# Making a block's weight low half before, and not after, the fetched row on VectorE

## The chip, the cores and the metric

One core of one Trainium2 chip runs the whole program. The metric is device time in microseconds (us) for one execution. TensorE is called PE in the profile, VectorE DVE, ScalarE ACT, GpSimd POOL and SyncE SP.

## What is computed

The program is two transformer blocks on 512 tokens of width 1024. The change lies in the last layer of the second one, a product-key mixture of 16384 experts (`peer`):

```
expert, gate: per token, 8 heads x 16 best of N_EXPERTS = 128 * 128
ub = u_tab[expert]; vb = v_tab[expert]          # rows of 1024
a  = gelu(einsum('td,ted->te', x, ub))          # 128 numbers per token
y  = einsum('te,ted->td', gate * a, vb)
```

The result is added to the residual stream.

## The kernel before

**Two ways to do the experts.** For tokens 0 to 383 the kernel multiplies the tokens with all 16384 rows of `peer_u`, in 128 blocks x of 128 experts each, and weighs the result with a gate matrix that is zero where a token did not choose an expert; a later stage multiplies the weighed result with `peer_v`. The last 128 tokens (one per partition) take the literal way: POOL fetches, for each of the 128 choices, the row of `peer_u` that each token chose (one indirect DMA into a ring `gathered` of NGATHER = 4 buffers), and DVE forms the dot product (`use_row`, L2308). Rows 128 to 255 are the rows of `peer_v`, which DVE adds up (L2316).

**Split weights.** Every block of weights arrives by SP's DMA in `wraw` (3 buffers), ACT makes its high half `WH` (L1191), and another engine its low half `WL = wraw - WH`. PE needs both and does three matmuls for each product (L469, L472, L473), 24 for one `u` block. From block FIRST_GATE_UP = 33 on, DVE makes the low halves (`low`, L2297); it must find the cast done (semaphore `w_hi`) and PE begun with the block two ahead of it in order (`w_begun`). PE waits for `WL` in `unit_views`; SP waits for the low half of unit u-3 before it reloads that `wraw` buffer.

**The gate stage** has blocks x = 33 to 127. In 64 of the first 86 of them PE also makes the gate matrices for four tokens (`gm`, L951) from one-hot matrices that DVE builds in two instructions (`hots_of`, L2329 and L2333). DVE's program is one loop over x, in a fixed order: one-hots for block x+1, one row, low half of block x+2. Two rows (EARLY = 2) are used ahead of the loop, so that 97 rows are used in this stage. Behind the loop `weigh(0)`, `weigh(1)` and `low_weighed(0)` prepare the first operands of the next stage, `down`.

**POOL's queue** is in one order too: a fetch of a row (L1160), then 0, 1 or 2 scatters of gate values to the gate matrices in DRAM (L1151; 128 in all, 16 over 11 rows), then the next fetch. Fetch r waits until row r-4 is used (`rows_used`). After the last scatter POOL loads four gate matrices, which `weigh` needs.

Of the kernel before, what the change touches and what calls it, by code (L numbers as in the profile page):

```python
# [68 lines left out]
FIRST_GATE_UP = 2 * PH * UP_BY_PART + UP_BEFORE_SEL + UP_AFTER_SEL  # L69
LAST_GATE_UP = FIRST_GATE_UP + GATE_UPS  # L70
NGATHER = 4
EARLY = 2
# [15 lines left out]
def fours_of(x):  # L88

    b = x - FIRST_GATE_UP  # L90
    if not 0 <= b < GATE_UPS:
        return range(0)
    fours = NFOUR - FIRST_FOUR
    return range(FIRST_FOUR + b * fours // GATE_UPS, FIRST_FOUR + (b + 1) * fours // GATE_UPS)


def rows_until(slot):

    ups = NEXP - FIRST_GATE_UP
    after = min(slot, GATE_UPS) + max(min(slot, ups) - GATE_UPS, 0)   # L100
    rest = 2 * HS - EARLY - ups
    return EARLY + after + min(max(slot - ups, 0) * rest // (NEXP - 4), rest)
# [34 lines left out]
def block_pair_kernel(nc, A, onehot_rows, inv_freq, out):  # L137

    ctx = ExitStack()
    with ctx:  # L140
# [5 lines left out]
        def s(name):  # L146
            if name not in sems:
                sems[name] = ctx.enter_context(nc.semaphore(name))
            return sems[name]
# [8 lines left out]
        def wait_full(eng, key):  # L158
            n = number[key]
            eng.wait_ge(s(f"full{n % 8}"), n // 8 + 1)  # L160
            return banks[n % 8]

        def wait_read(eng, key):

            n = number[key]
            eng.wait_ge(s(f"free{n % 8}"), n // 8 + 1)
# [6 lines left out]
        unit_at = {}  # L173
# [1489 lines left out]
        def _(dve):  # L1663
            links = [0]

            def link(ins):

                links[0] += 1
                ins.then_inc(s("dve_link"), 1)
                dve.wait_ge(s("dve_link"), links[0])  # L1670
# [619 lines left out]
            def low(u, made=s("w_low")):  # L2290
                if u >= len(units):
                    return
                k, n, _ = units[u]
                dve.wait_ge(s("w_hi"), u + 1)
                if u >= NW:
                    dve.wait_ge(s("w_begun"), u - NW + 2)
                dve.tensor_tensor(WL[:, u % NW, 0:k * n], wraw[:, u % NR, 0:k * n],  # L2297
                                  WH[:, u % NW, 0:k * n].bitcast(F32), ALU.subtract).then_inc(made, 1)

            def use_row(row):  # L2300
                dve.wait_ge(s(f"row_landed{row % NGATHER}"), 16 * (row // NGATHER + 1))
                at = gathered[:, row % NGATHER, :]
                if row == 0:
                    dve.wait_ge(s("x_nat_made"), 1)
                if row == HS:
                    dve.wait_ge(s("gates_copied"), 1)
                if row < HS:
                    dve.tensor_tensor_reduce(out=at, in0=at, in1=x_nat[:, :], scale=1.0, scalar=0.0, op0=ALU.mult, op1=ALU.add,  # L2308
                                             accum_out=gdot[:, row:row + 1]).then_inc(s("rows_used"), 1)
                    return  # L2310
                for n, (first, end) in enumerate(((0, UP_ROWS_1), (UP_ROWS_1, UP_ROWS_2))):
                    if row - HS == first:
                        dve.wait_ge(s("rows_active"), n + 1)
                        link(dve.tensor_tensor(gdot[:, first:end], gdot[:, first:end], ggate[:, first:end], ALU.mult))
                dve.wait_ge(s("rows_used"), row)
                dve.scalar_tensor_tensor(out=hN[:, NTD, :], in0=at, scalar=gdot[:, row - HS:row - HS + 1],  # L2316
                                         in1=hN[:, NTD, :], op0=ALU.mult, op1=ALU.add).then_inc(s("rows_used"), 1)

            def use_rows(slot):
                for row in range(rows_until(slot), rows_until(slot + 1)):  # L2320
                    use_row(row)

            def gate_matrices():
                def hots_of(x):
                    for four in fours_of(x):
                        if four >= FIRST_FOUR + NQ:
                            wait_full(dve, ("gm", four - NQ))
                        q, tok = four % NQ, slice(four * TOK4, (four + 1) * TOK4)
                        link(dve.tensor_tensor(hots[:, q, :, :, :],  # L2329
                                               iota128[:, :].unsqueeze(1).unsqueeze(1).to_broadcast([P, 2, TOK4, P]),  # L2330
                                               ijcol[:, :, tok].unsqueeze(3).to_broadcast([P, 2, TOK4, P]),
                                               ALU.is_equal))
                        dve.tensor_tensor(hots[:, q, 0, :, :], hots[:, q, 0, :, :],  # L2333
                                          gcol[:, tok].unsqueeze(2).to_broadcast([P, TOK4, P]), ALU.mult).then_inc(
                                              s("hots_made"), 1)

                low(LOW_BY_DVE)
                for t in range(TSCAT // P, NTD):
                    wait_read(dve, ("sel", t))
                hots_of(FIRST_GATE_UP)  # L2340
                low(LOW_BY_DVE + 1)
                for row in range(EARLY):
                    use_row(row)
                for x in range(FIRST_GATE_UP, NEXP):
                    hots_of(x + 1)
                    use_rows(x - FIRST_GATE_UP)
                    low(unit_at[("u", x)] + 2)
                for x in range(2):
                    weigh(x)
                low_weighed(0)  # L2350

            def weigh(x):
                dve.wait_ge(s(f"ag_landed{x % NAG}"), sum(32 if NAG <= n < SENT else 16 for n in range(x % NAG, x + 1, NAG)))
                if x < NAG:
                    dve.wait_ge(s("first_gates_landed"), 16 * NAG)
                if x >= 2:
                    dve.wait_ge(s("ga_lo"), x - 1)
                if x >= SENT:
                    wait_read(dve, ("a", x))
                if x == 0:  # L2360
                    for four in range(TSTAY // TOK4, NFOUR):
                        wait_read(dve, ("gm", four))
                a = ar[:, x % NAG, :] if x < SENT else kept[:, x - SENT, :]
                dve.tensor_tensor(ga[:, x % 2, 0:TSTAY], a[:, 0:TSTAY], gr[:, x % NAG, :], ALU.mult)
                dve.tensor_tensor(ga[:, x % 2, TSTAY:TD].rearrange("p (a t) -> p a t", a=NGSTAY),
                                  a[:, TSTAY:TD].rearrange("p (a t) -> p a t", a=NGSTAY), Gs[:, :, x, :],
                                  ALU.mult).then_inc(s("ga"), 1)

            def low_weighed(x):
                dve.wait_ge(s("ga_hi"), x + 1)  # L2370
                dve.tensor_tensor(GL[:, x % NGA, :], ga[:, x % 2, :], GH[:, x % NGA, :].bitcast(F32),
                                  ALU.subtract).then_inc(s("ga_lo"), 1)
# [24 lines left out]
            rows_and_norm(2, "norm2")  # L2397
            choose_experts()
            gate_matrices()
            down()  # L2400

# [56 lines left out]
```

## Time and profile before

| what | value |
|---|---|
| median of 3 runs | 2169.43 us |
| lowest, highest | 2164.5, 2172.26 us |
| span of the profiled execution | 2161.6 us |
| outside the span, to the median | 7.8 us |
| PE busy | 2121.7 us (98%) |
| DVE busy | 1442.4 us (67%) |
| POOL busy | 1038.6 us (48%) |
| gate stage in the profile | about 1166 to 1635.58 us |

The profiled execution has no time of its own in the results; its span covers the first to the last instruction, and the median stands 7.8 us above it. In a timeline row, the start and the duration of an instruction are followed by its engine, line, operation and tiles; in brackets stand the engine's idle time before it and what ended it.

### The profile page before, as it was taken

Reading aid. Unit: us, or ns where it says so; the run is one execution under the profiler, and the core shown is the slowest. Engines: PE = TensorE matmul, PEld = TensorE weight load, DVE = VectorE, ACT = ScalarE, POOL = GpSimd, SP = SyncE. Lnnn points to the kernel's source line nnn. Section 1 sums busy time; section 2 is a strip of 40 time slices with the busy share of each in tenths; the row PEclk is TensorE's granted clock in tenths of the full one; section 3 lists DMA queues with packets and bytes.
Section 4 is the critical chain, followed back from the end, with each engine's and each line's share of the span. In section 5 each row is a group of like instructions: output and inputs, shape, how many; then the busy total and the mean of one; then the engine's idle time right before and its main releaser. Section 6 shows DMA issues by size and latency. Waiting matters only on the chain.

```text
span 2161.6 us, 29125 instructions
## 1 busy us (share of the span) xinstructions
PE 2121.7 (98%) x10648; PEld 1837.8 (85%) x10648; DVE 1442.4 (67%) x2713; ACT 858.3 (40%) x1306; POOL 1038.6 (48%) x573
## 2 busy tenths in 40 slices
PE   8989999999999999999999999999999999999999
PEld 7857888888877877899999999999998888888887
DVE  5973411110054995369998777787867999999987
ACT  4354522232264454253334444444433333333332
POOL 1203244443423333435566888888863444444342
PEclk9999999999999999999999999999999999999999
DMA  4202344444442222334347899998899999999996
GB/s 177 82 27 62 104 117 127 117 119 115 117 118 74 86 71 77 117 106 121 112 147 207 242 267 321 284 315 249 261 309 318 388 388 371 373 375 377 369 359 251
DMA packets 240489, 444.14 MB, mean 205 GB/s; under 512 B 102459, under 2 KB 152028, under 8 KB 240220
## 3 DMA queue, kind: packets, MB, share of 16 engines
q1 hardware_dynamic: 152060, 299.07, 41.8%
q0 software_dynamic: 55488, 134.83, 19.3%
q10 hardware_dynamic: 32800, 8.39, 1.8%
q8 instruction: 85, 1.39, 0.3%
q14 instruction: 56, 0.46, 0.1%
HBM read 397.71 MB, written 44.50 MB: 205 GB/s over the span
## 4 chain that ended last, share of the span: by engine, by line
PE 69%; POOL 13%; DVE 8%; issue 4%; DMA 3%; ACT 2%; SPq 0%; DVEq 0%; ACTq 0%; POOLq 0%
PE bank L469 22%; PE bank L473 22%; PE bank L472 22%; POOL gate_matrices L1151 9%; POOL y L1160 4%; DMA y<-in_peer_u_rows,gidx 3%; DVE m L1979 1%; PE bank L923 1%; DVE xn L1980 1%; DVE WL L2297 1%; PE bank L645 1%; DMA wraw<-in_peer_u 1%; ACT sc L1302 1%; DVE y L2308 0%; DVE hots L2329 0%
## 5 line engine op out<-in xcount | busy, mean ns | idle before, releaser
L1140 POOL TENSOR_TENSOR WL<-wraw,WH 128x1024 fp32r<-128x1024 f32 x171 | 435.9, 2552 | 723.5 <-ACT WH L1191 723.5
L1191 ACT ACTIVATE WH<-wraw 128x1024 fp32r<-128x1024 f32 x411 | 435.0, 1060 | 627.4 <-PE bank L469 393.6
L469 PE MATMUL bank<-XH,WH 128*128 128x384 f32 (+2 forms) x1864 | 668.8, 359 | 12.6 <-DVE WL L2297 7.8
L473 PE MATMUL bank<-XH,WL 128*128 128x384 f32 (+2 forms) x1864 | 657.8, 353 | 0.0
L472 PE MATMUL bank<-XL,WH 128*128 128x384 f32 (+2 forms) x1864 | 657.6, 353 | 0.0
L469 PEld LDWEIGHTS bank<-XH,WH 128*128 128x128 f32 x1864 | 351.4, 189 | 46.3 <-issue 12.9
L472 PEld LDWEIGHTS bank<-XL,WH 128*128 128x128 f32 x1864 | 351.6, 189 | 29.0 <-issue 0.7
L473 PEld LDWEIGHTS bank<-XH,WL 128*128 128x128 f32 x1864 | 351.1, 188 | 28.7
L2297 DVE TENSOR_TENSOR WL<-wraw,WH 128x1024 fp32r<-128x1024 f32 x240 | 293.0, 1222 | 57.6 <-ACT WH L1191 51.8
L469 PE MATMUL bank<-WH,GH 128*128 128x512 f32 x768 | 298.9, 389 | 1.6 <-issue 1.6
L473 PE MATMUL bank<-WH,GL 128*128 128x512 f32 x768 | 298.8, 389 | 0.0
L472 PE MATMUL bank<-WL,GH 128*128 128x512 f32 x768 | 298.8, 389 | 0.0
L1160 POOL DMA_INDIRECT y<-in_peer_v,gidx x128 | 185.2, 1447 | 220.7 <-DVE hN L2316 203.0
L1151 POOL DMA_INDIRECT gate_matrices<-scat_gate,scat_at x128 | 243.7, 1904 | 40.9 <-issue 38.4
L2308 DVE CUSTOM_DVE_ANT_0 y<-y,x_nat 128x1024 f32<-128x1024 f32 x128 | 156.0, 1223 | 108.6 <-DMA y<-in_peer_u_rows,gidx 103.4
L1160 POOL DMA_INDIRECT y<-in_peer_u_rows,gidx x128 | 169.3, 1323 | 106.1 <-DVE gdot L2308 77.0
L469 PEld LDWEIGHTS bank<-WH,GH 128*128 128x128 f32 x768 | 144.1, 188 | 32.3 <-issue 2.3
L473 PEld LDWEIGHTS bank<-WH,GL 128*128 128x128 f32 x768 | 144.1, 188 | 29.9
L472 PEld LDWEIGHTS bank<-WL,GH 128*128 128x128 f32 x768 | 144.2, 188 | 29.8
L2316 DVE SCALAR_TENSOR_TENSOR hN<-y,gdot,hN 128x1024 f32<-128x1024 f32 x128 | 163.9, 1280 | 3.6 <-DMA y<-in_peer_v,gidx 0.6
L1589 ACT ACTIVATE ac<-bank 128x384 f32<-128x384 f32 x122 | 59.8, 490 | 239.0 <-PE bank L473 223.6
L1904 DVE TENSOR_TENSOR y<-bank,y 128x512 f32<-128x512 f32 x22 | 15.2, 692 | 208.2 <-PE bank L473 208.2
(313 smaller groups left out, 2561.8 us busy)
## 6 DMA issues: line engine op xcount, KB each, us to landing
wraw<-in_peer_u SPq DMA_DIRECT2D x128, 512.0 KB
wraw<-in_peer_v SPq DMA_DIRECT2D x128, 512.0 KB
activations<-ac SPq DMA_DIRECT2D x122, 192.0 KB
ar<-activations SPq DMA_DIRECT2D x122, 192.0 KB
gr<-gate_matrices SPq DMA_DIRECT2D x124, 128.0 KB
wraw<-in_w_gate SPq DMA_DIRECT2D x22, 512.0 KB
wraw<-in_w_up SPq DMA_DIRECT2D x22, 512.0 KB
wraw<-in_w_down SPq DMA_DIRECT2D x22, 512.0 KB
```

Of the source, the lines that this page charges most:

```text
L469: mm = pe.matmul(out, wh, xh, start=first, stop=False)
L472: pe.matmul(out, wh, xl, start=False, stop=False)
L473: return pe.matmul(out, wl, xh, start=False, stop=last)
L645: mm = pe.matmul(out[half, (h % 4) * P:(h % 4 + 1) * P], v1[:, b - 1 + kt, half], pT1[:, h, kt, :], start=kt == kts[0], stop=kt == 1)
L1140: pool.tensor_tensor(WL[:, u % NW, 0:m], wraw[:, u % NR, 0:m], WH[:, u % NW, 0:m].bitcast(F32), ALU.subtract).then_inc(s("w_lo"), 1)
L1151: pool.indirect_dma_start(out=gate_cells[:, :], out_offset=bass.IndirectOffsetOnAxis(ap=scat_at[:, k:k + 1], axis=0), in_=scat_gate[:, k:k ...
L1160: pool.indirect_dma_start(out=gathered[:, row % NGATHER, :], out_offset=None, in_=(u_rows if row < HS else v_rows)[:, :], in_offset=bass.I ...
L1191: act.activation(WH[:, u % NW, 0:k * n], wraw[:, u % NR, 0:k * n], ACT.Copy).then_inc(s("w_hi"), 1)
L1589: act.activation(ac[:, x % NAC, :] if x < SENT else kept[:, x - SENT, :], src[:, 0:TD], ACT.Gelu_apprx_tanh).then_inc(frees(("a", x)), 1)
L2297: dve.tensor_tensor(WL[:, u % NW, 0:k * n], wraw[:, u % NR, 0:k * n], WH[:, u % NW, 0:k * n].bitcast(F32), ALU.subtract).then_inc(made, 1)
L2308: dve.tensor_tensor_reduce(out=at, in0=at, in1=x_nat[:, :], scale=1.0, scalar=0.0, op0=ALU.mult, op1=ALU.add, accum_out=gdot[:, row:row + ...
L2316: dve.scalar_tensor_tensor(out=hN[:, NTD, :], in0=at, scalar=gdot[:, row - HS:row - HS + 1], in1=hN[:, NTD, :], op0=ALU.mult, op1=ALU.add) ...
```

## The change

In each pass of the loop the low half of block x+2 is made before the row and no longer after it. The two early rows, ahead of the loop before, are now used in the first pass, behind its low half. No instruction is added or removed, and the other engines' programs are the same.

```diff
                 hots_of(FIRST_GATE_UP)
                 low(LOW_BY_DVE + 1)
-                for row in range(EARLY):
-                    use_row(row)
                 for x in range(FIRST_GATE_UP, NEXP):
                     hots_of(x + 1)
+                    low(unit_at[("u", x)] + 2)
+                    if x == FIRST_GATE_UP:
+                        for row in range(EARLY):
+                            use_row(row)
                     use_rows(x - FIRST_GATE_UP)
-                    low(unit_at[("u", x)] + 2)
                 for x in range(2):
                     weigh(x)
                 low_weighed(0)
```

## Rows read from the trace of the kernel before

**Rows 1.** The page's chain that ended last, by engine.

```profile
PE 69%; POOL 13%; DVE 8%; issue 4%; DMA 3%; ACT 2%; SPq 0%; DVEq 0%; ACTq 0%; POOLq 0%
```

**Rows 2.** Busy time by stretch: stretch, us, engines busy (instructions), PEclk, DMA share, GB/s.

```profile
1166.00:1595.00 429.00, 423.78 (x2612) 422.85 (x2610) 324.51 (x395) 198.37 (x244) 361.11 (x217) 1.00 0.94 273
...
1640.00:2161.00 521.00, 518.35 (x2286) 428.60 (x2284) 470.58 (x698) 186.00 (x254) 221.89 (x154) 1.00 0.97 361
```

**Rows 3.** Waits from 1166 to 1595 us: total us, times, longest us.

```profile
DVE y L2308 <- DMA y<-in_peer_u_rows,gidx: 96.3, 56, 5.6
...
PE bank L469 <- DVE WL L2297: 5.2, 4, 2.4
...
POOL y L1160 <- DVE gdot L2308: 4.0, 13, 0.3
...
DVE WL L2297 <- ACT WH L1191: 0.7, 1, 0.7
```

**Rows 4.** Timeline of DVE, one pass of the loop.

```profile
1315.12 1.23 DVE L2308 CUSTOM_DVE_ANT_0 y<-y,x_nat 128x1024 f32<-128x1024 f32 x1 [1.72 <-DMA y<-in_peer_u_rows,gidx]
...
1316.27 1.22 DVE L2297 TENSOR_TENSOR WL<-wraw,WH 128x1024 fp32r<-128x1024 f32 x1
1317.41 1.22 DVE L2329 TENSOR_TENSOR hots<-iota,sq 128x1024 f32<-128x1024 f32 x1
...
1319.32 1.21 DVE L2308 CUSTOM_DVE_ANT_0 y<-y,x_nat 128x1024 f32<-128x1024 f32 x1
```

**Rows 5.** Timeline of PE, starts of blocks and of the next stage.

```profile
1209.43 0.49 PE L469 MATMUL bank<-XH,WH 128*128 128x384 f32 x1 [2.38 <-DVE WL L2297]
...
1317.64 0.41 PE L469 MATMUL bank<-XH,WH 128*128 128x384 f32 x1 [0.49 <-DVE WL L2297]
...
1322.70 0.42 PE L469 MATMUL bank<-XH,WH 128*128 128x384 f32 x1
...
1603.08 0.41 PE L469 MATMUL bank<-XH,WH 128*128 128x384 f32 x1 [0.73 <-DVE WL L2297]
...
1635.58 0.47 PE L469 MATMUL bank<-WH,GH 128*128 128x512 f32 x1 [1.63 <-issue]
```

**Rows 6.** Instruction groups from 1166 to 1595 us, POOL's two.

```profile
L1151 POOL DMA_INDIRECT gate_matrices<-scat_gate,scat_at x128 | 243.7, 1904 | 40.9 <-issue 38.4 <-DMA gate_matrices<-scat_gate,scat_at 2.5
...
L1160 POOL DMA_INDIRECT y<-in_peer_u_rows,gidx x89 | 117.6, 1321 | 30.3 <-issue 22.9 <-DVE gdot L2308 4.0 <-DVE gidx L2277 3.5
```

**Rows 7.** Timeline of DVE at the stage's end.

```profile
1600.56 1.22 DVE L2308 CUSTOM_DVE_ANT_0 y<-y,x_nat 128x1024 f32<-128x1024 f32 x1 [5.14 <-DMA y<-in_peer_u_rows,gidx]
...
1601.71 1.22 DVE L2297 TENSOR_TENSOR WL<-wraw,WH 128x1024 fp32r<-128x1024 f32 x1
...
1628.28 1.22 DVE L2308 CUSTOM_DVE_ANT_0 y<-y,x_nat 128x1024 f32<-128x1024 f32 x1
...
1631.29 1.23 DVE L2297 TENSOR_TENSOR WL<-wraw,WH 128x1024 fp32r<-128x1024 f32 x1 [1.79 <-ACT WH L1191]
1633.28 0.42 DVE L2364 TENSOR_TENSOR ga<-ar,gr 128x256 f32<-128x256 f32 x1 [0.76 <-issue]
...
1634.92 0.56 DVE L2371 TENSOR_TENSOR GL<-ga,GH 128x384 fp32r<-128x384 f32 x1 [0.48 <-ACT GH L1637]
```

**Rows 8.** Timeline of ACT: the cast that the low half at 1601.71 needs.

```profile
1600.24 1.06 ACT L1191 ACTIVATE WH<-wraw 128x1024 fp32r<-128x1024 f32 x1 [5.05 <-DMA wraw<-in_peer_u]
```

**Rows 9.** Busy time by stretch, columns as in Rows 2: the block after the longest stall.

```profile
1209.00:1213.00 4.00, 3.57 (x12) 3.60 (x13) 3.97 (x6) 1.06 (x1) 3.39 (x3) 0.58 0.79 151
```

**Rows 10.** Timeline of POOL: a scatter beside a low half, scatter and fetch beside idle DVE.

```profile
1239.43 2.54 POOL L1151 DMA_INDIRECT gate_matrices<-scat_gate,scat_at  x1 [0.31 <-issue]
...
1245.79 1.55 POOL L1151 DMA_INDIRECT gate_matrices<-scat_gate,scat_at  x1 [0.30 <-issue]
1247.64 1.00 POOL L1160 DMA_INDIRECT y<-in_peer_u_rows,gidx  x1 [0.30 <-issue]
```

**Rows 11.** Timeline of DVE at the first of these scatters.

```profile
1239.32 1.21 DVE L2297 TENSOR_TENSOR WL<-wraw,WH 128x1024 fp32r<-128x1024 f32 x1
```

## The prediction

> **What bounds the kernel now.** I read first the busy time by stretch. PE is busy for 423.78 of 429 us while the gate stage's scatters run, and for 518.35 of 521 us in the last stage [rows 2]. So PE sets the end, the last stage follows PE's own pace, and an edit in the gate stage is worth what it takes from PE's gaps there, plus what it does to the moment at which the last stage starts.
>
> Then the waits of that stretch. PE waited 4 times for a low half, 5.2 us in all, while DVE waited 96.3 us for fetched rows [rows 3]. The low half stands behind the row on DVE, so a late row makes a late low half. The timeline shows one such case: the row is there at 1315.12, its low half starts at 1316.27, and PE starts the block at 1317.64 after 0.49 us idle [rows 4, 5]. From row to low half it is 1.15 us, from the start of the low half to PE 1.37 us, and 2.52 us in all.
>
> Last, who sets the pace of the rows. The chain of waits gives POOL 13% of the span [rows 1], although it is busy for half of it. In the 429 us POOL's two kinds of instruction are busy for 243.7 + 117.6 us, and nearly all of the 71.2 us before them is a fixed issue gap: its waits for a used row are 4.0 us in 13 pieces of 0.3 us, which is that same gap [rows 3, 6]. So POOL's queue is full from 1166 to 1595 us, the rows come at its pace, and PE, a little faster, is dragged by it whenever a row is late. This is why the four stalls cannot simply be added up as a gain.
>
> **The change part by part.** *Low half ahead of the row, in the steady loop.* The same instructions run. A low half now waits for the row of the pass before, and one-hots stand between them. After the row at 1315.12 would come its 1.15 us, then the one-hots, 1.91 us (1317.41 to 1319.32), then the low half of the block that PE starts at 1322.70 [rows 4, 5]. That block could begin at 1315.12 + 1.15 + 1.91 + 1.37 = 1319.55, so it has 3.15 us to spare, where its forerunner had none. The general form: one block period with gates, 5.06 us (1317.64 to 1322.70), less 1.91 us. A block without gates has no one-hots, and the room is larger. With the rows coming when they did, PE can therefore run 3.15 us earlier and no more before it waits for the rows again. I take 3.15 us as the gain at 1595 us. Its ends: nothing, if some other input of PE has no room; and all that the stalls cost there, 5.2 us plus the slow block after the longest of them. That block shows a granted clock of 0.58 over 4 us, so mostly the lower level of 1.2 GHz, after PE had been idle for 2.38 us [rows 5, 9]; (1 - 0.58) x 4 = 1.7 us. The upper end is 6.9 us.
>
> *The rows themselves* move back by one low half, up to 1.15 us. In this stretch that costs nothing: POOL asks for row r-4 before it fetches row r, and does not wait for it beyond its issue gap [rows 3]. That cover is gone only after 1595 us, where no scatter is left and POOL has time to spare. *SP's reload* of a `wraw` buffer waits for a low half, which comes no later, so the streams are not delayed. *What a low half newly queues:* the row, and with it POOL's ring, now stand behind its wait for the cast. Over the 429 us that wait was met once, for 0.7 us [rows 3]. *The two early rows* go behind the low half of block 35 and the first stall goes with them; it is one of the four and is already in the sum.
>
> *The end of the scatters.* A row arrives at 1600.56, its low half starts at 1601.71 and PE is stalled until 1603.08 [rows 5, 7]. The cast was started at 1600.24 and takes 1.06 us [rows 8]; a low half behind the cast alone could start at 1601.33. It gains 0.4 us.
>
> *The last pass.* Here the change costs. Before: row at 1628.28, the low half waits for its cast until 1631.29, then `weigh(0)` after 0.76 us in which DVE only issues waits, and PE starts the last stage at 1635.58 after a stall of 1.63 us, right behind the low weighed half at 1634.92 [rows 5, 7]. Afterwards the last row, which had lain in DVE's idle time ahead of that cast, stands between the low half and `weigh(0)`. Nothing hides it, because PE is already waiting for this chain: +1.15 us, and the stall becomes 2.8 us. The SP loads behind `weigh(0)` and the next stage's start all move with it, so it is counted once.
>
> Sum: -3.15 - 0.4 + 1.15 = -2.4 us. Against the profiled span: 2161.6 - 2.4 = 2159.2; with the 7.8 us that the median stands above the span, 2167.0 us.
>
> **The rivals.**
>
> *The clock falls before the last stage.* The stall of 2.8 us is longer than the one of 2.38 us after which the clock was at 1.2 GHz; the one of 1.63 us was followed by matmuls at full pace. If it falls for as long, it costs 1.7 us again [rows 5, 9]: 2168.7 us. The Trainium skill ("TensorE: Matmul & The Clock Gate", Part 1) has the clock gate slow PE when it has been idle, and the case at 1209.43 agrees. By that rule the last stage would start slow and the time would be this rival's; since only one stall here shows it, and others of 1.63 us do not, I give it less than even.
>
> *POOL's pace changes, against us.* A scatter that starts 0.1 us into a low half takes 2.54 us, one beside an idle DVE 1.55 us [rows 10, 11]. The means are 1.904 us for 128 scatters and 1.321 us for 89 fetches, against 1.55 and 1.00 us for the undisturbed: 128 x 0.35 + 89 x 0.32 = 45 + 28 = 73 us of POOL's queue is stretch that depends on how its instructions fall on DVE's [rows 6, 10]. Now the order on DVE is one-hots, low half, row. If a POOL instruction leaves the one-hots and meets the low half more often, the rows slow down and PE, which has only the room worked out above, slows with them one for one. The low half adds as much blocking as before, which speaks against it; the fact that the two blockers lay back to back, and now lie 0.7 us apart (1.91 less the 1.22 us of the first one-hot instruction) [rows 4], speaks for it. One more stretch of 1 us at every eighth of the 88 rows is 11 us: -2.4 + 11 = +8.6, 2178 us. It turns a gain to a loss from 2.4 us on, and beyond 0.3% from 8.9 us on, an eighth of the stretch there is.
>
> The Trainium skill speaks on this ("SBUF — State Buffer", the sections on ports): a DVE instruction with two SBUF inputs holds off a GpSimd one that reads SBUF, whichever comes second. By that rule the row instruction would hold POOL off as well, DVE's order would hardly matter, and this rival's extra would be nothing; the trace agrees for the low half.
>
> *POOL's pace changes, for us.* The same in the other direction. With 3.8 us or more taken from the queue the stalls all go and PE gains the whole 6.9 us: -6.9 - 0.4 + 1.15 = -6.1, 2163.3 us. It can't go much further, since nothing else of PE's time is touched.
>
> *The moved low half brings nothing.* PE's stalls could fall back on another input (the cast, a late stream), and only the cost at the end stays: +1.15, 2170.6 us. Against it: DVE waited for a cast once in this stretch, and the rows explain each stall.
>
> **How the numbers follow.** The forecast, 2167.0 us, has 42%; the clock 20% (2168.7); POOL's pace shorter 14% (2163.3); no gain 10% (2170.6); POOL's pace longer 14% (from 2170 to 2178). The least and greatest of the likely cases are 2163.3 and about 2172; the three runs shown differ by 7.8 us, so I add about 2 us on either side: 2161.5 to 2174.0. It leaves out the upper part of the slow rival and a little below. A measurement can tell some 0.3%, 6.5 us, from no change. Faster by more needs nearly the whole 6.1 us and luck in the medians: 11%. Slower by more is the upper part of POOL's longer pace: 13%. Within: 76%.
>
> **What would show it right or wrong.** PE's waits for the low half between 1166 and 1595 us should vanish for block 35 and sum up to some 2 to 4 us less with the slow block gone; PE's last stage should start 2 to 3 us earlier, near 1633 us, behind a stall of 2.8 us and not 1.63 us, with the row right in front of `weigh(0)`. The last scatter should stand within a few us of where it stood; if it moved by more, POOL's pace decides the result. The scatter and fetch means should stay near 1.90 and 1.32 us. I am wrong if POOL's waits for used rows appear before 1595 us, if the low halves wait for casts there, or if the last stage no longer keeps PE's own pace.

## The result, and the profile after

The changed kernel takes 2156.55 us (median of 14 runs, 2153.34 to 2160.82), the kernel before 2164.71 us on the same chip (14 runs, 2161.49 to 2177.38). The ratio is 0.9948, 95% interval 0.9935 to 0.9961: 0.5% faster. The forecast was 2167.0 us with a range of 2161.5 to 2174.0, and faster had a chance of 0.11. The prediction was wrong.

In the runs here the time is 1.7 to 2.2 us above the span, in most of them 1.9 to 2.1; the profiled run of the changed kernel took 2159.24 us with a span of 2157.3. The "7.8 us that the median stands above the span" was therefore about 2 us outside the span and nearly 6 us of difference between runs: three runs had given a median of 2169.43, fourteen give 2164.71.

The chain of waits has lost its POOL part, 13% before [rows 1]:

```profile
PE 89%; DVE 7%; ACT 2%; DMA 1%; issue 1%; SPq 0%; DVEq 0%; ACTq 0%
```

Busy time by stretch, columns as in [rows 2]. The scatters now end at 1589 us, and PE is busy for the whole of 424.00 us while they run; the last stage is as it was:

```profile
1166.00:1590.00 424.00, 424.00 (x2630) 423.96 (x2629) 326.51 (x398) 199.01 (x246) 355.83 (x218) 1.00 0.95 278
...
1635.00:2156.00 521.00, 518.52 (x2287) 428.85 (x2285) 469.94 (x698) 186.42 (x254) 227.65 (x154) 1.00 0.97 361
```

The waits up to 1590 us. PE's line of [rows 3], 5.2 us for low halves, has no successor. DVE waits less for rows (81.0 us, 96.3 before), and the low halves wait for casts 9 times where they did once, since DVE now gets ahead:

```profile
DVE y L2308 <- DMA y<-in_peer_u_rows,gidx: 81.0, 48, 4.4
...
DVE WL L2297 <- ACT WH L1191: 13.6, 9, 4.6
...
POOL y L1160 <- DVE gdot L2308: 1.2, 4, 0.3
```

POOL's two groups from 1166 to 1595 us. Scatters last as long as before (1904 ns), fetches 74 ns less than 1321 [rows 6]:

```profile
L1151 POOL DMA_INDIRECT gate_matrices<-scat_gate,scat_at x128 | 243.9, 1906 | 40.7 <-issue 38.1 <-DMA gate_matrices<-scat_gate,scat_at 2.6
...
L1160 POOL DMA_INDIRECT y<-in_peer_u_rows,gidx x90 | 112.2, 1247 | 27.8 <-issue 25.6 <-DVE gdot L2308 1.2 <-DVE gidx L2277 0.7
```

The first fetch and the last scatter of POOL's list, in the timeline of the kernel before and then of the changed one. From the start of the one to the end of the other it is 1593.46 - 1166.13 = 427.3 us before and 1589.04 - 1168.01 = 421.0 us after:

```profile
1166.13 1.16 POOL L1160 DMA_INDIRECT y<-in_peer_u_rows,gidx  x1 [3.49 <-DVE gidx L2277]
...
1591.38 2.08 POOL L1151 DMA_INDIRECT gate_matrices<-scat_gate,scat_at  x1 [0.30 <-issue]
```

```profile
1168.01 1.16 POOL L1160 DMA_INDIRECT y<-in_peer_u_rows,gidx  x1 [0.67 <-DVE gidx L2277]
...
1586.70 2.34 POOL L1151 DMA_INDIRECT gate_matrices<-scat_gate,scat_at  x1 [0.30 <-issue]
```

The end of the stage: PE's first matmul of the last stage, then DVE, then ACT, of the changed kernel:

```profile
1630.74 0.47 PE L469 MATMUL bank<-WH,GH 128*128 128x512 f32 x1 [1.63 <-issue]
...
1626.46 1.23 DVE L2297 TENSOR_TENSOR WL<-wraw,WH 128x1024 fp32r<-128x1024 f32 x1 [1.79 <-ACT WH L1191]
1627.60 1.22 DVE L2308 CUSTOM_DVE_ANT_0 y<-y,x_nat 128x1024 f32<-128x1024 f32 x1
...
1628.74 0.42 DVE L2365 TENSOR_TENSOR ga<-ar,gr 128x256 f32<-128x256 f32 x1
...
1630.08 0.56 DVE L2372 TENSOR_TENSOR GL<-ga,GH 128x384 fp32r<-128x384 f32 x1
...
1629.15 0.49 ACT L1589 ACTIVATE kept<-bank 128x384 f32<-128x384 f32 x1 [2.72 <-PE bank L473]
1629.53 0.98 ACT L1637 ACTIVATE GH<-ga 128x384 fp32r<-128x384 f32 x2
```

I measure the whole stage from DVE's `gidx` instruction (L2277), which starts the fetches, to this matmul: 470.0 us before (1165.55 to 1635.58), 463.3 us after (1167.43 to 1630.74), 6.7 us less. The profiled run of the changed kernel reached the stage 1.9 us later than that of before.

PE's busy time in these two stretches, before and then after (columns as in [rows 2]), parts the 6.7 us: 5.2 us less idle (470.03 - 461.32 = 8.7 us before, 463.31 - 459.80 = 3.5 us after) and 1.5 us less work, which fits the one spell at the lower clock that the kernel before had here:

```profile
1165.55:1635.58 470.03, 461.32 (x2823) 459.37 (x2823) 348.25 (x429) 212.56 (x264) 377.58 (x233) 1.00 0.93 279
```

```profile
1167.43:1630.74 463.31, 459.80 (x2832) 458.89 (x2831) 348.11 (x429) 212.59 (x265) 371.26 (x233) 1.00 0.94 282
```

### The profile page after: what moved, and what is told of

Same layout as the page of the kernel before. It is cut to its first block, busy times and chain, and to the rows that moved or that the text cites. A ratio compares the mean times of both kernels' runs of the same rounds, so it can differ in the third digit from the quotient of the medians.

```text
span 2157.3 us, 29125 instructions
## 1 busy us (share of the span) xinstructions
PE 2123.1 (98%) x10648; PEld 1840.5 (85%) x10648; DVE 1439.8 (67%) x2713; ACT 858.0 (40%) x1306; POOL 1039.3 (48%) x573
## 4 chain that ended last, share of the span: by engine, by line
PE 89%; DVE 7%; ACT 2%; DMA 1%; issue 1%; SPq 0%; DVEq 0%; ACTq 0%
PE bank L469 27%; PE bank L473 27%; PE bank L472 27%; PE bank L951 3%; DVE m L1979 1%; DMA wraw<-in_peer_u 1%; PE bank L645 1%; PE bank L923 1%; DVE xn L1980 1%; ACT sc L1302 1%; PE bank L860 0%; DMA wraw<-in_w_in 0%; DVE sc L1838 0%; DVE isc L1980 0%; PE bank L592 0%
## 5 line engine op out<-in xcount | busy, mean ns | idle before, releaser
L1160 POOL DMA_INDIRECT y<-in_peer_v,gidx x128 | 189.7, 1482 | 212.7 <-DVE hN L2316 196.5
L1160 POOL DMA_INDIRECT y<-in_peer_u_rows,gidx x128 | 163.9, 1281 | 104.2 <-DVE gdot L2308 75.5
```

Of the source, the lines that this page charges most:

```text
L1160: pool.indirect_dma_start(out=gathered[:, row % NGATHER, :], out_offset=None, in_=(u_rows if row < HS else v_rows)[:, :], in_offset=bass.I ...
```

## The experiments

Two theories stood against each other at first. By A, my prediction's own, the low half had no room behind its row, and room is what the new order gives. By B, the order of the blocking instructions on DVE sets POOL's pace. Later ones sharpen B to C, given below.

**Where in the order the gain lies.** The first runs part the change in two and move the low half further.

The loop's new order, with the early rows left ahead of the loop:

```diff
+                for row in range(EARLY):
+                    use_row(row)
                 for x in range(FIRST_GATE_UP, NEXP):
                     hots_of(x + 1)
                     low(unit_at[("u", x)] + 2)
-                    if x == FIRST_GATE_UP:
-                        for row in range(EARLY):
-                            use_row(row)
                     use_rows(x - FIRST_GATE_UP)
```

> The loop's new order, with the two early rows left ahead of the loop as before. Theory A (the low half no longer waits for the row of its own pass, so PE's stalls behind late rows go): nearly the whole gain, 6 to 8 us below the kernel before; the first stall (1.70 us at block 35) shrinks too, because the low half of block 35 no longer waits for row 2. Theory B (the gain comes from the first pass, where the early rows stood in front of everything): at most 2 us.

Only the first pass changed, the other passes as before:

```diff
-                    low(unit_at[("u", x)] + 2)
                     if x == FIRST_GATE_UP:
+                        low(unit_at[("u", x)] + 2)
...
                     use_rows(x - FIRST_GATE_UP)
+                    if x > FIRST_GATE_UP:
+                        low(unit_at[("u", x)] + 2)
```

> Only the first pass is changed (low half of block 35, then rows 0, 1 and 2); every later pass keeps the row in front of the low half. Theory A: the first stall of 1.70 us goes, but the rows still come at POOL's pace and PE meets them at the next block, so 0 to 2 us are gained and waits of 3 to 5 us for the low half remain. Theory B: 6 to 8 us gained.

The low half first of all, ahead of the one-hots (the order is low half, one-hots, row):

```diff
-                    hots_of(x + 1)
                     low(unit_at[("u", x)] + 2)
+                    hots_of(x + 1)
```

> Order low half, one-hots, row: the low half has 1.9 us more room than in the changed kernel, but low half and one-hots lie back to back on DVE again, as before the change. Theory A1 (room alone): as fast as the changed kernel or up to 1 us faster, no waits of PE for a low half before 1595 us. Theory A2 (part of the gain is POOL's shorter queue, since the two operations that hold POOL off no longer lie back to back): POOL needs 427 us from its first fetch to its last scatter as before, instead of 421 us; PE still has room (3.15 + 1.9 us), so that only 1 to 2 us of the gain are lost.

The changed kernel once more:

> The changed kernel once more, for a second profile beside the others on one chip. Both theories: 7 to 11 us below the kernel before. If POOL's shorter queue (421 us) is an effect of the order it is there again, within 2 us; if it was chance, it lies anywhere between 420 and 430 us. PE's stall before the last stage is 1.63 us again, because ACT's cast for that stage stands behind the eviction of block 127.

| run | median (range), us | ratio, 95% interval | POOL's list, us | stage, us |
|---|---|---|---|---|
| e1, loop only | 2157.72 (2154.12 to 2161.19) | 0.9957 (0.9942 to 0.9972) | 421.2 | 464.3 |
| e2, first pass only | 2166.74 (2160.1 to 2176.37) | 0.9998 (0.9979 to 1.0017) | 427.0 | 472.5 |
| e3, low half first | 2170.25 (2161.44 to 2173.4) | 1.001 (0.9991 to 1.0029) | 432.0 | 477.0 |
| e4, changed kernel | 2158.07 (2153.63 to 2162.79) | 0.9962 (0.995 to 0.9975) | 420.9 | 463.9 |

"POOL's list" is the stretch from the first fetch to the end of the last scatter. The whole gain is the loop's order; the early rows bring nothing that the runs can tell (e1 against e4). And e3 speaks against A: the low half is earliest there and PE never waits for it up to 1595 us, yet nothing is gained. By itself it doesn't settle A, for its waits up to 1595 us show that the stall went to another input, the one-hots, which are now last before the row; e6 below does:

```profile
PE bank L951 <- DVE hots L2333: 8.3, 7, 2.2
```

**The row first.** The next runs repeat the kernel before, turn the loop to row, one-hots, low half, and take POOL out of the way by leaving out every second scatter.

The kernel before once more, one run:

> The kernel before, profiled again. It tells which stalls are of the kernel and which of one execution. Theory A: 4 to 7 us of waits of PE for low halves before 1595 us, most of it in the first ten blocks, and at least one spell of halved clock behind one of over 2 us. POOL from its first fetch to its last scatter: 425 to 430 us if the order sets it.

The row ahead of the one-hots:

```diff
+                for row in range(EARLY):
+                    use_row(row)
                 for x in range(FIRST_GATE_UP, NEXP):
+                    use_rows(x - FIRST_GATE_UP)
                     hots_of(x + 1)
                     low(unit_at[("u", x)] + 2)
-                    if x == FIRST_GATE_UP:
-                        for row in range(EARLY):
-                            use_row(row)
-                    use_rows(x - FIRST_GATE_UP)
```

> Order row, one-hots, low half: the low half waits for the row of its own pass and for the one-hots, 1.9 us later than in the kernel before. Theory A: the dragging by the rows grows by what was 3.15 us of room in the changed kernel, turned round: 2 to 4 us slower than the kernel before, PE waits for low halves of 6 to 10 us. Theory B (room plays no part, the order only changes how POOL falls on DVE): within 1 us of the kernel before.

Half of the scatters left out, in the kernel before and in the changed one:

```diff
+                if k % 2:
+                    return
...
-                    pool.wait_ge(s("scattered"), 16 * k)
+                    pool.wait_ge(s("scattered"), 8 * k)
...
-                    pool.wait_ge(s("scattered"), 16 * HS)
+                    pool.wait_ge(s("scattered"), 8 * HS)
```

> The kernel before with every second scatter left out (64 of 128), so that POOL has some 140 us to spare in the stage; the gate matrices of the first 128 tokens lack half their entries. Theory A: the rows are never late, PE waits for no low half, and the time falls by 6 to 8 us, to that of the changed kernel. Rival (rows are late because of the DMA engines' load, not POOL's queue): waits for low halves of 3 us or more remain.

> The changed kernel with every second scatter left out in the same way. Theory A: with POOL out of the way the order is worth nothing: within 1 us of the kernel before with half its scatters. If the new order has a price of its own at the end of the stage (the prediction's 1.15 us), it shows here alone, as 1 us slower than that one.

| run | median (range), us | ratio, 95% interval | POOL's list, us | stage, us |
|---|---|---|---|---|
| e5, kernel before | 2175.19, one run | | 436.6 | 484.6 |
| e6, row first | 2158.76 (2154.76 to 2166.4) | 0.9958 (0.9939 to 0.9977) | 421.2 | 466.4 |
| e7, before, half scatters | 2155.7 (2153.48 to 2161.09) | 0.9937 (0.9914 to 0.9961) | 402.0 | 467.5 |
| e8, changed, half scatters | 2156.14 (2153.51 to 2161.14) | 0.9946 (0.9925 to 0.9966) | 405.1 | 462.2 |

The order of e6 puts the low half behind the row and the one-hots, with less room than in the kernel before, and has the full gain. So A is wrong in both directions. With half of POOL's scatters gone the medians of the old and the new order are equal within 0.5 us (e7 and e8, whose intervals are each about 0.2% to either side), so as far as they can tell the whole gain comes through POOL's list. The changed kernel has little more to win from it: e8 is 2 us below e4, with intervals that overlap. Two limits: fewer scatters are also less DMA traffic, which no run took apart; and the profile of e7, its slowest run, still has a stage 5.3 us longer than that of e8. There PE waits once for a low half, 2.24 us ahead of 1182.45 us, for block 35, where the early rows stand in front of it (1.70 us in the kernel before), and once for 2.01 us behind the last scatter, each time with a spell at the lower clock. In the 386 us from the first of these to the last scatter the old order with half of the scatters has no such wait.

e5 also shows how much the old order varies: its stage was 14.6 us longer than in the profiled run of before. PE was idle for 16.0 us of it and had three spells at the lower clock, 5.1 us in all; some 4 us of the difference are not accounted for. It has 9 waits for low halves up to 1595 us, and another 6.4 us of them behind the last scatter, where the kernel before has 1.8 us and the changed one 1.9 us:

```profile
PE bank L469 <- DVE WL L2297: 7.1, 9, 2.2
```

**What holds POOL.** Set side by side, the timelines of the two engines show a plain law: a POOL fetch or scatter that starts while one of DVE's long instructions of this stage runs (all have two SBUF inputs) takes longer by the time for which that one still runs. That holds for the low half, as I had read, and for the first one-hot instruction and for the row too; the short second one-hot instruction is seldom met, but where it was, 9 times in ten profiles more than 0.1 us after its start and well before its end, it held POOL as well, by 0.10 to 0.48 us. A case of the kernel before that I had missed: a row runs from 1324.01 to 1325.16, a scatter starts 0.73 us into it, with 0.42 us of it left, and takes 0.36 us more than the 1.57 us of one that nothing holds:

```profile
1324.01 1.23 DVE L2308 CUSTOM_DVE_ANT_0 y<-y,x_nat 128x1024 f32<-128x1024 f32 x1 [0.43 <-DMA y<-in_peer_u_rows,gidx]
...
1324.74 1.93 POOL L1151 DMA_INDIRECT gate_matrices<-scat_gate,scat_at  x1 [0.30 <-issue]
```

From there the order follows, and this is theory C. In most profiles a row holds POOL more often than any other instruction (55 of 127 holds in e5, though 34 of 107 in the profile of before); that this is because it starts whenever its data land is my reading. Released at its end, POOL starts its next instruction about 1.26 us later after a fetch and 1.83 us later after a scatter, counted from the start of the next DVE instruction. In the order row, low half, one-hots the next two starts on DVE lie 1.14 us later (first one-hot instruction) and 2.39 us later: POOL falls 0.12 or 0.69 us into a 1.25 us instruction, and is held again. In the order row, one-hots, low half they lie 1.25 us later (second one-hot instruction) and 1.86 us later (low half): POOL meets both almost exactly at a boundary, and goes free, since the hold begins only some 0.04 us after a start (last section). What counts is the cycle, not its first member; so e3 is the old order, and e6 the new one.

C was put to three kinds of kernel. First, the new order with the low half between the two one-hot instructions, so that a third long instruction follows right on two others:

```diff
-                def hots_of(x):
+                def hots_of(x, between=None):
...
-                        link(dve.tensor_tensor(hots[:, q, :, :, :],
+                        made = step(dve.tensor_tensor(hots[:, q, :, :, :],
...
+                        if between:
+                            between()
+                        dve.wait_ge(s("dve_link"), made)
...
+                    if between and not len(fours_of(x)):
+                        between()
...
-                    hots_of(x + 1)
-                    low(unit_at[("u", x)] + 2)
+                    hots_of(x + 1, lambda: low(unit_at[("u", x)] + 2))
```

> The changed kernel with the low half put between the two one-hot instructions, so that row, first one-hot and low half follow each other on DVE without the second one-hot instruction (0.6 us, which never held a POOL instruction in the traces) among them. Theory C (a POOL fetch or scatter that starts while a row, a low half or a first one-hot runs is held until that instruction ends, and in an unbroken run of three of them a held one leads to the next being held): POOL needs 427 us or more from first fetch to last scatter, PE waits for low halves again, and the gain is lost, within 3 us of the kernel before. Theory A (what counts is that the low half is ahead of the row): the gain stays, 8 us or more below the kernel before.

Then the kernel before with an extra short instruction (128x512) between low half and one-hots:

```diff
+                gap = []
...
                     low(unit_at[("u", x)] + 2)
+                    if x + 2 < NEXP:
+                        if gap:
+                            dve.wait_ge(s("dve_link"), gap[-1])
+                        gap.append(step(dve.tensor_tensor(xn[:, 0, :].rearrange("p (a n) -> p a n", a=TOK4),
+                                          iota128[:, :].unsqueeze(1).to_broadcast([P, TOK4, P]),
+                                          gcol[:, 2 * P:2 * P + TOK4].unsqueeze(2).to_broadcast([P, TOK4, P]), ALU.mult)))
```

> The kernel before with an extra DVE instruction of the second one-hot's size between the low half and the next one-hots (into a tile nobody reads), in every pass but the last two. If it holds POOL as little as that one, theory C: POOL needs 421 to 424 us, and 5 to 9 us are gained in spite of 0.6 us more work in each pass. Theory A: the low half is still behind the row and DVE has more to do: 1 to 5 us slower than the kernel before.

And both kernels with each low half of this stage in two instructions of half the columns:

```diff
-                dve.tensor_tensor(WL[:, u % NW, 0:k * n], wraw[:, u % NR, 0:k * n],
-                                  WH[:, u % NW, 0:k * n].bitcast(F32), ALU.subtract).then_inc(made, 1)
+                cut = k * n // 2 if unit_at[("u", FIRST_GATE_UP)] + 2 <= u <= unit_at[("e", 1)] else 0
+                if cut:
+                    dve.tensor_tensor(WL[:, u % NW, 0:cut], wraw[:, u % NR, 0:cut],
+                                      WH[:, u % NW, 0:cut].bitcast(F32), ALU.subtract)
+                dve.tensor_tensor(WL[:, u % NW, cut:k * n], wraw[:, u % NR, cut:k * n],
+                                  WH[:, u % NW, cut:k * n].bitcast(F32), ALU.subtract).then_inc(made, 1)
```

> The kernel before with the low half of the gate stage made in two instructions of 512 columns each. Theory C: what a POOL instruction can be held by a low half is halved, POOL needs 5 to 10 us less than the 427 to 437 us of the kernel before, and 6 to 10 us are gained. Theory A: the extra instruction costs DVE 0.1 us a pass and nothing is gained.

> The changed kernel with the same split of the low half. Theory C: POOL needs less than the changed kernel's 421 us, but PE does not wait for it there any more, so the time stays within 2 us of the changed kernel's. If it is faster than that by more, POOL's queue still cost something in the changed kernel.

| run | median (range), us | ratio, 95% interval | POOL's list, us | stage, us |
|---|---|---|---|---|
| e9, low half between | 2172.09 (2168.52 to 2179.92) | 1.0017 (1.0001 to 1.0033) | 437.8 | 479.7 |
| e10, before, extra instruction | 2184.25 (2183.01 to 2190.77) | 1.0074 (1.005 to 1.0099) | 444.1 | 490.9 |
| e11, before, split low halves | 2164.21 (2159.17 to 2175.54) | 0.9978 (0.9962 to 0.9995) | 428.1 | 471.7 |
| e12, changed, split low halves | 2157.36 (2155.58 to 2159.55) | 0.9943 (0.9921 to 0.9966) | 417.0 | 463.0 |

e9 agrees with C: the low half is still made ahead of the next row, and the gain is gone. The expectation's aside that the second one-hot instruction never held POOL was not quite so (four holds of 0.10 to 0.48 us in the profiles up to then, seven in e9). Its timeline of DVE, and then of POOL, shows the repeated hold. A scatter starts 0.18 us into the row and is held until 1321.71; the fetch behind it starts 0.69 us into the low half and is held again, for 0.40 us above its 1.00 us:

```profile
1320.56 1.22 DVE L2308 CUSTOM_DVE_ANT_0 y<-y,x_nat 128x1024 f32<-128x1024 f32 x1 [0.40 <-DMA y<-in_peer_u_rows,gidx]
...
1321.71 1.22 DVE L2329 TENSOR_TENSOR hots<-iota,sq 128x1024 f32<-128x1024 f32 x1
1322.85 1.22 DVE L2297 TENSOR_TENSOR WL<-wraw,WH 128x1024 fp32r<-128x1024 f32 x1
1323.98 0.68 DVE L2336 TENSOR_TENSOR hots<-hots,rt 128x512 f32<-128x512 f32 x1
...
1320.74 2.49 POOL L1151 DMA_INDIRECT gate_matrices<-scat_gate,scat_at  x1 [0.30 <-issue]
1323.54 1.40 POOL L1160 DMA_INDIRECT y<-in_peer_u_rows,gidx  x1 [0.30 <-issue]
```

e10 was to space the long instructions out, on the condition that the extra one holds POOL little. The condition failed, and the run went against the expected sign. Its timeline tells why. Low half and extra instruction take 1.74 us, so POOL's start 1.81 us after a row-held scatter falls 0.07 us into the first one-hot instruction and is held for nearly the whole of it (DVE first, then POOL). The extra instruction itself holds POOL too, 24 times for 10.5 us in all, so that e10 shows the cost of both together:

```profile
1313.87 1.23 DVE L2308 CUSTOM_DVE_ANT_0 y<-y,x_nat 128x1024 f32<-128x1024 f32 x1 [0.57 <-DMA y<-in_peer_u_rows,gidx]
...
1315.03 1.22 DVE L2297 TENSOR_TENSOR WL<-wraw,WH 128x1024 fp32r<-128x1024 f32 x1
1316.16 0.69 DVE L2352 TENSOR_TENSOR xn<-iota,rt 128x512 f32<-128x512 f32 x1
1316.77 1.22 DVE L2329 TENSOR_TENSOR hots<-iota,sq 128x1024 f32<-128x1024 f32 x1
...
1314.35 2.19 POOL L1151 DMA_INDIRECT gate_matrices<-scat_gate,scat_at  x1 [0.30 <-issue]
1316.84 2.02 POOL L1160 DMA_INDIRECT y<-in_peer_u_rows,gidx  x1 [0.30 <-issue]
```

C's beat can be counted in all the timelines. Of POOL's instructions that a row held, and whose next followed at once, so many had that next one held too, at the mean (zeros counted):

| cycle on DVE | kernel | row held, then held again | mean, us |
|---|---|---|---|
| row, low half, one-hots | before, e5, e2, e3, e11 | 25 of 34, 41 of 54, 36 of 50, 37 of 49, 36 of 50 | 0.46 in before |
| row, one-hot, low half, one-hot | e9 | 48 of 61 | 0.47 |
| row, low half, extra, one-hots | e10 | 42 of 51 | 0.70 |
| row, one-hots, low half | changed, e1, e4, e6 | 4 of 54, 3 of 50, 4 of 41, 1 of 51 | 0.03 in changed |

That is 175 of 237 against 12 of 196. Rows hold POOL no less often in the new order; what is gone is the second hold. The holds add up to what POOL's list lost: what its instructions took above 1.00 or 1.57 us, counted from 0.05 us on, is 70.5 us before, 78.8 us in e5 and 64.5 us in the changed kernel, so that 6.0 of the list's 6.3 us between the first and the last of these are holds. The counts were made after the runs. For e10, where the forecast had the other sign, they explain the result and confirm no expectation; e9 is the run that C, against A, forecast rightly.

e11 is a half miss. C expected 5 to 10 us less of POOL's list; it stayed at 428.1, within what the old order shows between runs (427.0 to 436.6), and the 0.2% that it gained has an interval that nearly touches 1. By the beat this fits: a split low half takes the same time altogether, so POOL's next start falls into the first one-hot instruction as before and is held again (36 times of 50 with the few that met another row). e12 shortened the list once more, by 4 us, and not the time: its interval and e4's overlap, and e8 had shown the same. No version beats the changed kernel by more than the measurement tells.

## Why the prediction was wrong

**What bounds the kernel: right.** PE sets the end, POOL's list was full from 1166 to 1595 us, and PE was dragged by it. What I didn't work out is how near the two paces lie. PE needs 5.06 us for a block with gates [rows 5] and 4.17 us for one without (the usual periods in the timeline of the changed kernel, where nothing stalls it), (64 x 5.06 + 22 x 4.17) / 86 = 4.83 us a block. POOL needs 427.3 / 88 = 4.86 us for a row in the profiled run of before, 436.6 / 88 = 4.96 in e5, and 421.0 / 88 = 4.78 in the changed kernel. Before, POOL is the slower by 0.5 to 2.7%; after, it is the faster by 1%. What could be won was what PE lost to POOL's lateness in stalls and slow clock, and hardly more: in the changed kernel PE is idle for 3.5 us of the stage, 1.63 us of them ahead of the last stage.

**The steady loop: the step that failed.** The sum allowed 3.15 us, "with the rows coming when they did". They didn't: the change takes 6.3 us from POOL's list, and the stalls (5.2 us) and the slow block (1.7 us) all go, the 6.9 us that I had as the upper end. The case was on the list as "POOL's pace changes, for us", at 14% and with a price of -6.1 us; the stage became 6.7 us shorter. The room that I had worked out is real but decides nothing: e3 has more of it and gains nothing, e6 has less and gains all.

**What holds POOL: read wrong, and with it the chances.** I took low half and one-hots for the blockers and argued only over their distance. I had the 73 us of stretch, and that it "depends on how its instructions fall on DVE's", but named only two of the three long kinds they fall on. In ten profiles (before, changed, e1 to e6, e9, e10) 461 POOL instructions started at least 0.1 us after a row's start and 0.1 us ahead of its end, and what they took above 1.00 or 1.57 us is what the row had left, with a mean difference of 0.05 us; for 264 beside a low half it is 0.08 us, for 262 beside a first one-hot instruction 0.13 us. The Trainium skill ("SBUF — State Buffer", Terms) has the shared port pair held for the full instruction, and these agree. What I had drawn from that page, that the row holds POOL as well, is right; that it goes for "whichever comes second" shows here in one direction only, with POOL the one that waits (last section); and that "DVE's order would hardly matter" is not right, for the order decides whether POOL's next start meets a boundary.

**The end of the scatters, -0.4 us: of no weight here.** There PE waits for a late stream of weights in both kernels, 0.73 + 1.11 us before and 0.48 + 1.40 us after. The sum had only the first of these waits. Over all profiles they are not alike: with all scatters they come to 1.8 to 6.4 us where POOL's list took 427 us or more, and to 1.6 to 2.4 us where it took 421.2 us or less. Why a slow list goes with a late stream no run shows.

**The last pass, +1.15 us: nil, and so was the rival on the clock.** "Nothing hides it, because PE is already waiting for this chain" was wrong, and a row shown before spoke against it: `GL` at 1634.92 waits 0.48 us for ACT [rows 7]. ACT can make `GH` only behind its eviction of PE's last `u` block. Its timeline of before has this already:

```profile
1633.98 0.49 ACT L1589 ACTIVATE kept<-bank 128x384 f32<-128x384 f32 x1 [2.72 <-PE bank L473]
1634.37 0.92 ACT L1637 ACTIVATE GH<-ga 128x384 fp32r<-128x384 f32 x2
```

After the change the row stands in front of `ga`, as forecast, but the 0.76 us in which DVE issued waits now pass while the row runs (1628.74 follows it without a gap), and what is left is less than ACT's own lateness. PE's stall is 1.63 us in every profile of the study, never 2.8 us, and the clock does not fall there.

**The median.** Two errors of base stand beside the sum: the 7.8 us, and a single profile for a kernel whose stage varied from 470.0 to 484.6 us between two profiles. The profiled run of before lay below the kernel's median (2161.6 + 2.0 against 2164.71 here, and 2167.54 to 2170.3 beside the experiments); against its span the changed kernel's is 4.3 us shorter, by the medians of 14 runs the time is 8.2 us shorter. The rival's own 2163.3 us missed by 6.8 us for that reason: on a base of 2161.6 + 2.0 it would have been 2157.5.

Open: no kernel was tried that changes the beat and leaves everything else alone, such as a delay on POOL by itself; and none that takes the scatters' DMA traffic away and leaves POOL's time as it is.

## What to carry to other kernels

When two engines run at nearly the same pace, divide each one's stretch by its number of units first (here 4.83 and 4.86 us): the gain of an edit is set by which becomes slower, and not by the room of a single wait. Where one engine's instructions hold another's to their end, follow one release through the next two starts of each order; a cycle whose sums (1.25 and 1.86 us) match the other's intervals (1.26 and 1.83 us) costs nothing, and one that is off by 0.07 us (e10, after a scatter) can cost nearly a whole instruction (1.02 us in the case shown, 0.70 us at the mean). Before a row is called uncovered at a stage's end, look which engine ends last in the wait of the next instruction, and take the base from many runs, not from one profile.

## What the runs showed of the hardware

- An indirect DMA on POOL that starts inside one of this stage's DVE instructions with two SBUF inputs takes longer by what that one has left: 1.00 us for a fetch and 1.57 us for a scatter when free, up to 2.1 and 2.6 us when held. The edge is sharp: over ten profiles none of 126 that started up to 0.03 us after the start of a row, low half or one-hot instruction (92 of them at a second one-hot instruction) was held by more than 0.3 us, and all of 131 that started 0.05 to 0.10 us after that of a row, low half or first one-hot instruction were. That is why a beat that is off by 0.05 us can cost a microsecond.
- No sign of the hold the other way: some 2,340 row, low half and first one-hot instructions of these stretches, nearly all with a POOL instruction under way, took 1.21 to 1.30 us. The fetch at 1247.64 [rows 10] shows the same from POOL's side: a row starts at 1248.00, in its midst, and it takes its 1.00 us.
- POOL's list in the new cycle took 421.0, 421.2, 420.9 and 421.2 us in four profiles of three kernels, that of the old 427.0 to 436.6 in five: one order repeats within 0.3 us, the other varies by 9.6 us.
- A stall of PE of about 2 us may or may not bring the clock down. Over the fourteen profiles, 12 of the 18 stalls of 2.0 to 4.2 us in this stage went with a spell at the lower clock of 1.2 GHz, among them one of 2.01 us (e7); 6 did not, among them 2.39 us (e4) and 2.56 us (e6). No stall of 1.70 us or less did, that of 1.63 us ahead of the last stage included. A spell cost 1.7 us each time, and 3.4 us behind the stall of 3.86 us in e3.
